# Query parts made a step ahead, and in the dilated units the transposes of the probabilities two steps behind the scores

## The reference

```python
h = _rms_norm(x, norm_attn_g)
qa, ka, va, fa, qb, kb, vb, ga, gb = split(h @ w_in)
oa = _fox_attention(qa, ka, va, log_sigmoid(fa + b_forget))     # 8 heads of 64, causal, forgetting bias
ob = _dilated_mixture(rope(qb), rope(kb), vb)                   # 12 heads: 4 each at dilation 1, 4, 16
mixed = sigmoid(ga) * (oa @ w_branch_a) + sigmoid(gb) * (ob @ w_branch_b)
x = x + mixed @ w_out
x = x + square(relu(_rms_norm(x, norm_mlp_g) @ w_up)) @ w_down
return _rms_norm(x, norm_final_g)
```

## Time and profile before

| | |
|---|---|
| time, median of 3 runs | 1677.96 us (1674.87 to 1681.14) |
| profiled execution, own time | 1677.7 us |
| its span, first to last instruction | 1675.9 us |
| TensorE busy | 1552.0 us, 93% |
| DVE busy | 1094.3 us, 65% |
| ACT busy | 782.0 us, 47% |
| dilated units | about 71 to 383 us of the span |
| forgetting units | about 413 to 690 us |
| granted TensorE clock, mean | 0.98 of full |

### The profile page before, as it was taken

One profiled execution on the slowest core, in us unless ns is written; L12 is line 12 of the kernel. 1 busy time (PEld: TensorE's weight loads), 2 busy tenths in 40 slices (PEclk: granted clock), 3 DMA queues, 4 the chain that ended last, 5 costly groups with the idle time before them and its releaser, 6 DMA issues. The chain is left out here.

```text
span 1675.9 us, 20825 instructions
## 1 busy us (share of the span) xinstructions
PE 1552.0 (93%) x7436; PEld 1277.8 (76%) x7436; DVE 1094.3 (65%) x1775; ACT 782.0 (47%) x1396; POOL 4.1 (0%) x20
## 2 busy tenths in 40 slices
PE   6998888897789998899999999999999899999997
PEld 5777677775677786788888887888888677777776
DVE  5687878866566666523225567666666677777776
ACT  6466666662556656511113454343343444444442
POOL 0000000000000000000000000000000000000000
PEclk9999999999899999999999999999999999999998
DMA  5210100110010201111211543444444784444412
GB/s 176 89 39 26 38 26 26 28 37 13 13 51 26 76 26 36 36 48 44 56 55 55 151 126 94 151 144 167 163 149 151 248 285 138 140 138 144 139 39 101
DMA packets 161584, 154.45 MB, mean 92 GB/s; under 512 B 7048, under 2 KB 126920, under 8 KB 161360
## 3 DMA queue, kind: packets, MB, share of 16 engines
q1 hardware_dynamic: 161488, 153.19, 28.9%
HBM read 115.35 MB, written 37.81 MB: 91 GB/s over the span
## 5 line engine op out<-in xcount | busy, mean ns | idle before, releaser
L942 PE MATMUL ps<-hspl,wsp 128*128 128x512 f32 x1536 | 428.9, 414 | 5.4 <-ACT tmp L1356 3.7
L942 PEld LDWEIGHTS ps<-hspl,wsp 128*128 128x128 f32 x1536 | 270.8, 193 | 52.2 <-ACT tmp L1356 4.6
L1233 PE MATMUL ps<-dn_b,a_hi 128*128 128x512 f32 x896 | 280.0, 394 | 17.5 <-DVE keep L2022 11.8
L898 PE MATMUL ps<-hspl,wsp 128*128 128x512 f32 x960 | 220.7, 390 | 1.4 <-DVE keep L1869 1.4
L1233 PEld LDWEIGHTS ps<-dn_b,a_hi 128*128 128x128 f32 x896 | 168.0, 189 | 59.3 <-issue 24.1
L898 PEld LDWEIGHTS ps<-hspl,wsp 128*128 128x128 f32 x960 | 179.7, 188 | 38.6 <-issue 1.6
L1233 PE MATMUL ps<-dn_b,a_lo 128*128 128x512 f32 x448 | 175.8, 392 | 0.0
L2022 DVE TENSOR_TENSOR keep<-keep,ps 128x512 f32<-128x512 f32 (+1 forms) x144 | 101.5, 713 | 38.2 <-PE ps L1233 24.5
L1233 PE MATMUL ps<-up_b,a_hi 128*128 128x512 f32 x384 | 119.6, 393 | 3.7 <-DVE up_b L2022 2.7
L1855 DVE TENSOR_TENSOR work<-ps,work 128x128 fp32r<-128x128 f32 (+3 forms) x144 | 59.1, 420 | 72.3 <-ACT work L1401 70.2
L1604 ACT ACTIVATE keep<-keep 128x512 f32<-128x512 f32 x64 | 40.5, 633 | 125.9 <-DVE keep L2184 42.8
(11 more groups left out here) (211 smaller groups left out, 2560.8 us busy)
## 6 DMA issues: line engine op xcount, KB each, us to landing
hidden<-keep SPq DMA_DIRECT2D x112, 256.0 KB, 2.2
dn_raw<-hidden SPq DMA_DIRECT2D x56, 512.0 KB, 6.4
raw<-in_w_in SPq DMA_DIRECT2D x47, 512.0 KB, 3.8
a_raw<-in_w_up SPq DMA_DIRECT2D x36, 256.0 KB, 3.0
a_raw<-in_w_down SPq DMA_DIRECT2D x32, 256.0 KB, 3.0
spare<-in_w_down SPq DMA_DIRECT2D x32, 256.0 KB, 4.2
spare<-in_w_up SPq DMA_DIRECT2D x28, 256.0 KB, 3.2
keep<-in_x SPq DMA_DIRECT2D x8, 512.0 KB, 7.0
```

The lines of the kernel that those rows point to most:

```text
L898: ins = pe.matmul(ps[:, cols], w(wp, k), mv(mp, k)[:, cols], start=(k == 0 and n == 0), stop=(k == ks - 1 and n == 2))
L942: ins = pe.matmul(psp(u, g), wsp[c % 2][:, wp, k * P:(k + 1) * P], hspl[:, mp, k, cols], start=(n == 0), stop=(n == 23), skip_group_check= ...
L1233: ins = pe.matmul(o, a_part(n, j, wp, k), b_block(n, j, mp, k), start=(first and k == 0 and m == 0), stop=(k == ks - 1 and m == 2), skip_g ...
```

## The change

No instruction is added or taken away in sum. Three things change.

1. `query_ops(G)` says which query parts a step makes: part 0 of block `B` in step `2B - 3`, part 1 in `2B - 2`, one step ahead of before. A unit's first block is made whole in step 14 and step 13 makes none. On ACT the query part now stands behind `exps` and `probs_hi`. Ahead of the loop one more query part is made.
2. In the dilated units (`late` = 1) the transposes, both parts of the probabilities, the values, the outputs and the values' transposes each move one step back: `transposes(G - 2)` in step `G`, outputs in odd steps instead of even ones, `value_transposes` in step 2 instead of 1.
3. Probabilities of the dilated units have a third buffer, `probs_third`, and `exps(G)` waits for `transposes(G - 3)`. In the forgetting units these things stay.

```diff
@@ -185,6 +185,14 @@
     return [(i - 1, None), (i, None)]
 
 
+def query_ops(G):
+
+    B, n = (G + 1) // 2 + 1, (G + 1) % 2
+    if G % STEPS == 13 or G == STEPS * N_DIL - 1 or B >= BLOCKS * MIX:
+        return []
+    return [(B, 0), (B, 1)] if G % STEPS == 14 or G == STEPS * N_DIL else [(B, n)]
+
+
 def tiles_of(G):
     return key_tiles(G // STEPS, query_tile(G % STEPS))
 
@@ -262,6 +270,7 @@
         fbias = [at(f"fbias{i}", [P, 2, S], F32, 196 + 8 * i) for i in range(2)]
 
         q_fox = at("q_fox", [P, 2, 2, 2 * P], F32R, 192)
+        probs_third = at("probs_third", [P, 2 * P], F32, 92)
         pt_odd = at("pt_odd", [P, 2048], F32R, 128)
 
         up_b = [at(f"up_b{j}", [P, 2, 4, HALF], F32R, 64 + 16 * j) for j in range(3)]
@@ -379,7 +388,7 @@
         def probs(G):
 
             if G < STEPS * N_DIL:
-                return tmp[:, 6, HALF + (G % 2) * 256:HALF + (G % 2 + 1) * 256]
+                return probs_third[:, :] if G % 3 == 2 else tmp[:, 6, HALF + (G % 3) * 256:HALF + (G % 3 + 1) * 256]
             return tmp[:, G % 2, :]
 
 
@@ -1025,22 +1034,23 @@
                         ins.then_inc(vt_done, 1)
 
             def mixer_steps(first, last):
-                for G in range(first, last + 2):
+                late = 0 if first else 1
+                for G in range(first, last + 2 + late):
                     if G < last:
                         scores(G)
                     if G < last:
                         project_part(G, 0)
-                    if first <= G - 1 < last:
-                        transposes(G - 1)
+                    if first <= G - 1 - late < last:
+                        transposes(G - 1 - late)
                     if G < last:
                         project_part(G, 1)
                     if G < last:
                         project_part(G, 2)
-                    if G % 2 and first <= G - 3 < last:
+                    if (G - late) % 2 and first <= G - 3 - late < last:
                         if G % STEPS == 1 and first:
                             inverse_rows(G // STEPS - N_DIL - 1)
-                        values((G - 3) // 2)
-                    if G % STEPS == 1 and G < last:
+                        values((G - 3 - late) // 2)
+                    if G % STEPS == 1 + late and G < last:
                         value_transposes(G // STEPS)
 
             for g in range(6):
@@ -1387,7 +1397,7 @@
             def exps(G):
                 n = len(tiles_of(G))
                 act.wait_ge(max_done, G + 1)
-                after(act, tr_done, units_before(G - 1))
+                after(act, tr_done, units_before(G - 1 if G > STEPS * N_DIL else G - 2))
                 act.activation(probs(G)[:, 0:n * P], psc[G % 2][:, 0:n * P], ACT.Exp,
                                bias=stat(G, 0), scale=-1.0, accum_out=stat(G, 1)).then_inc(exp_done, 1)
 
@@ -1416,24 +1426,25 @@
                 act.copy(o_part[row:row + 64, :], o_bank(B)[64 - row:P - row, :]).then_inc(op_done, 1)
 
             def mixer_steps(first, last):
-                for G in range(first, last + 3):
+                late = 0 if first else 1
+                for G in range(first, last + 3 + late):
                     t, s = divmod(G, STEPS)
                     if group_out(t, s) is not None and G < last:
                         raw_evacuate(t + 1, group_out(t, s))
                     if s == 0 and G > first:
                         raw_evacuate(t, 5 if t < MIX else 3)
-                    if G % 2 == 0 and first <= G - 4 < last:
+                    if (G - late) % 2 == 0 and first <= G - 4 - late < last:
                         if s == 2 and first:
                             inverse_rows(t - N_DIL - 1)
-                        out_part((G - 4) // 2)
-                    if G < last and G // 2 + 1 < BLOCKS * MIX:
-                        query_hi(G // 2 + 1, G % 2)
+                        out_part((G - 4 - late) // 2)
                     if G < last:
                         exps(G)
-                    if first <= G - 1 < last:
-                        probs_hi(G - 1)
+                    if first <= G - 1 - late < last:
+                        probs_hi(G - 1 - late)
                     if G < last:
-                        if s == 1:
+                        for B, n in query_ops(G):
+                            query_hi(B, n)
+                        if s == 1 + late:
                             values_hi(t)
                         if s == (0 if t == N_DIL else 2):
                             split_hi(CH0 + 3 * t + 4)
@@ -1459,6 +1470,7 @@
             query_hi(0, 0)
             query_hi(0, 1)
             raw_evacuate(0, 5)
+            query_hi(1, 0)
             mixer_steps(0, STEPS * N_DIL)
 
 
@@ -1896,22 +1908,24 @@
                 return jobs
 
             def mixer_steps(first, last):
-                for G in range(first, last + 3):
+                late = 0 if first else 1
+                for G in range(first, last + 3 + late):
                     t, s = divmod(G, STEPS)
-                    if G % 2 == 0 and first <= G - 4 < last:
-                        outs((G - 4) // 2)
+                    if (G - late) % 2 == 0 and first <= G - 4 - late < last:
+                        outs((G - 4 - late) // 2)
                     jobs = side_work(G) if G < last else []
                     if G < last:
                         maxes(G)
                     for job in jobs[:1]:
                         job()
-                    if first <= G - 1 < last:
-                        probs_lo(G - 1)
+                    if first <= G - 1 - late < last:
+                        probs_lo(G - 1 - late)
                         if first and G > first and s == 0:
                             inverses(t - N_DIL - 1)
-                    if G < last and G // 2 + 1 < BLOCKS * MIX:
-                        query_lo(G // 2 + 1, G % 2)
-                    if s == 1 and G < last:
+                    if G < last:
+                        for B, n in query_ops(G):
+                            query_lo(B, n)
+                    if s == 1 + late and G < last:
                         values_lo(t)
                     for job in jobs[1:]:
                         job()
@@ -1926,6 +1940,7 @@
             split_lo(4)
             query_lo(0, 0)
             query_lo(0, 1)
+            query_lo(1, 0)
             mixer_steps(0, STEPS * N_DIL)
 
 
```

## The result

The changed kernel takes 1682.94 us (median of 7 runs, 1681.05 to 1688.02), the kernel before beside it 1678.29 us (7 runs, 1673.76 to 1681.14): a ratio of 1.0039, 95% interval 1.0022 to 1.0055. The forecast of no change on the slow side, 1684 us, holds. Not all of its terms do: its two halves, for the dilated and the forgetting units, were off by some 5.5 us each, in opposite directions.

What follows compares the result with a forecast made beforehand. The prediction took the DVE-ACT round trip to bound the dilated units, not TensorE. Its terms, -10.4 + 1.5 + 10.9 + 7.5 + 1.0 - 2.1 - 2.3 = +6.1 on 1677.7 us, gave 1684 us; range 1660 to 1698.

Steps and rivals of the forecast that it cites:

- The thesis: Dilated units: TensorE's 24.3 us of query waits mostly shadow a DVE-ACT loop, which an earlier TensorE doesn't shorten.
- Query part behind the cast on ACT, +10.9: Dilated units: DVE's query part must wait for ACT's later query cast; +10.9 us, bounds 0 and 15.
- Outputs in odd steps, and step 3, +8.5: Dilated units: DVE waits for output parts queued on ACT; +7.5 us for step 9, +1.0 for step 3.
- What an earlier TensorE gives in the dilated units, -4.4: Dilated units: score waits after halved-clock steps go, -2.1 us; step 3's exp no longer stands behind the query cast, -2.3.
- Forgetting units, -10.4 + 1.5: Forgetting units: earlier query parts remove DVE's score waits, -10.4 us; first step and dilated stretch's later drain add +1.5.
- TensorE's waits whole, 1636 us: Both stretches: TensorE's query waits, 41.8 us, come back whole: 1636 us; chance 0.17, from 1636 to 1667.
- Dilated costs hidden, 1667 us: DVE catches up in each unit's last steps, so only the forgetting units' -10.4 stays: 1667 us; chance 0.15.
- The clock, 1701 us: Dilated units: TensorE's idle time gathers at steps 9 and 10, lowering its clock; 17 us more, 1701 us; chance 0.16.

Runs made afterwards that it cites:

- one_behind: q_first_dil with transposes, probabilities, values and outputs one step behind, in two buffers, as before the change; ratio 0.9950 to the kernel before.
- dilated_only: Dilated units as in the change, forgetting units as in the kernel before; ratio 1.0058 to the kernel before.
- outs_behind2: The change with both output halves moved behind in the dilated units, ACT's copy behind its query part; ratio 0.9969 to the kernel before.
- q_first_dil: The change, but ACT makes its query part ahead of the exp in the dilated units; ratio 0.9972 to the kernel before.
- q_first_all: The change, but ACT makes its query part ahead of the exp in all units; ratio 0.9920 to the kernel before.

## Why the prediction was right, and where it was wrong

**The thesis held for the waits it was about.** TensorE's waits for query parts in the dilated units were mostly the shadow of a loop through DVE and ACT. They went from 24.3 to 6.0 us and the stretch grew by 9.7 us. DVE's idle time grew to 79.0 us, where under 60 would have refuted it. By that loop's own account, the idle time ahead of DVE's groups against the earlier trace rows: max 9.9 to 1.1 us, probabilities 36.1 to 30.8, output 12.8 to 17.1, -9.8 in sum, and the query part up to 25.2 from next to nothing. DVE's idle time follows the stretch; TensorE's waits for query parts don't. But not all of the growth is that loop's own: 6.3 of the 9.7 us are slower products on TensorE, for which the sum has no term.

**Query part behind the cast on ACT, +10.9.** Right: 11.9 us between the kernels that differ in it, 9.5 of them idle time. The waits per step were right too (0.39 us for 0.37). Their total was not, 23.0 us instead of 11; since the maxes and probabilities are waited for 14.1 us less, part of it only changed its place.

**Outputs in odd steps, and step 3, +8.5: the waits right, the price not shown.** There are four waits of 1.54 to 1.78 us in step 9 (1.7 forecast), 0.79 in unit 0 (0.7), 1.02 in step 3 (1.2). But other waits for output parts went, and their total is 16.2 us, where the prediction had some 25 (11.9 before). The second step behind as a whole costs 7.1 us, near the 8.5, and that nearness is luck: 6.9 of the 7.1 are slower products, not waits for the output. It was not foreseen that taking the outputs off the loop altogether gives up to 14 us, 8.4 of them by the clock.

**What an earlier TensorE gives in the dilated units, -4.4: the sign right, too small.** With one step behind and the query ahead, the stretch is 336.9 us against 346.9 (means of two kernels each): -10.0. The step that failed is "most others are at the start, before there is a lead". I kept 6.8 of DVE's 8.9 us of waits for scores; in one_behind 1.0 is left:

```profile
L1864 DVE CUSTOM_DVE_ANT_0 ps<-ps,dil_bias 128x128 f32<-128x128 f32 (+1 forms) x96 | 34.7, 361 | 1.9 <-PE ps L991 1.0
```

Of the 10.0 us, 6.8 are TensorE's idle time and 3.2 its busy time; the three falls of the clock in the kernel before, for which the prediction took 2.1 us, are gone in one_behind. The rest was not traced to single waits.

**Forgetting units, -10.4 + 1.5: this term was mis-sized, -3.3 measured.** DVE's waits for scores did fall as forecast, 12.3 to 1.5 us, and with ACT's query ahead the stretch shrinks by 12.0 us (263.2 to 251.2), so the gain was there. The step that failed is the sentence on ACT: that the high query part behind the cast is hidden, because DVE's part of 512 columns is longer. DVE's query part does not wait, but it isn't the only one behind that cast. At the head of the next step stands the emptying of the bank, and TensorE, which now comes early, waits for it: 3.2 us before, 17.0 after. The prediction named who waits for a moved instruction, and left out who waits for what is queued behind it. The Trainium skill, "PSUM — Partial Sum Buffer", section "Engine vs sequencer instructions", has ScalarE's queue as strictly first in, first out; the rows of unit 8 agree, with the bank's copy 0.58 us later for a query cast of 0.41.

**The sum.** -10.4 + 1.5 + 15.0 = +6.1 was forecast. The trace has -3.3 in the forgetting and +9.7 in the dilated stretch, +1.0 ahead of them, and -2.1 behind them, where the code is the same: +5.3. Both halves were some 5.5 us off, in opposite directions. That the sum is closer than its parts is luck.

**The rivals.** TensorE's waits whole, 1636 us: no kernel came near, though the mended one takes 24 us less than before; it gets them only with ACT's query part left ahead of the exp and the transposes one step behind. Dilated costs hidden, 1667 us: excluded by dilated_only. The clock, 1701 us: the mechanism took place, where the prediction had put it, and was priced too high. TensorE's lead does gather its idle time in one piece near step 10, as in unit 2:

```profile
212.82 0.68 PE L1023 MATMUL ps<-work 128*128 128x256 f32 x4 [3.31 <-DVE work L1867]
```

In the dilated loop of the change the clock falls to its lower level six times (at 156, 214, 234, 272, 292 and 330 us), before it three times, and not at all in outs_behind2 and one_behind. Each of the six begins within 1.5 us of the end of a wait of TensorE of 2.1 to 3.3 us: four for the values near step 10, two for the bank at the head of a unit. The rival had ten stretches and 17 us; the trace has three more than before and 6.3 us more of busy time. In the forgetting units it is not the clock that tells the change from what came before: TensorE's busy time there is 230.5 us, 233.6 before.

## What to carry to other kernels

Price a moved wait on the engine whose waits add up to the stretch, not on the busiest one: here TensorE's 41.8 us of waits for DVE were worth 10.0 + 12.0 us once nothing else was moved for the worse, and in the change 18 of them went in the dilated units while the stretch grew by 9.7 us. When an instruction moves within an in-order queue, list what stands behind its new place until the next wait, and ask for each who waits for it. When a change moves several things at once, undo them one at a time: making the query parts a step ahead was worth 22 us here, and what came with it cost 28.7 (ACT's order 11.9 and 9.7, the second step behind 7.1). And divide a stretch into TensorE's busy and idle time before you explain it by waits: where the same products take longer, ask for the clock, and look for the long pieces of idle time ahead of its falls.

## What the hardware showed that was not expected

A wait of 1.14 us left TensorE's granted clock at 1.00 and one of 2.25 us was followed by 4 us at 0.58, at the same place of the program. The wait of 2.26 us in the earlier trace rows was followed by 0.57. So a delay of half a microsecond on ACT was followed by two projection products of 1.22 instead of 0.73 us.

The length of the wait alone does not decide it. In q_first_dil and q_first_all, at the same place of the same code, TensorE waits 2.88 and 2.87 us; over the 4 us from there the granted clock is 0.64 in the one and 1.00 in the other:

```profile
210.27 0.68 PE L1023 MATMUL ps<-work 128*128 128x256 f32 x4 [2.88 <-DVE work L1871]
210.20:214.20 4.00, 3.93 (x15) 3.27 (x16) 3.77 (x11) 2.80 (x7) 0.00 (x0) 0.64 0.01 2
```

```profile
210.83 0.68 PE L1023 MATMUL ps<-work 128*128 128x256 f32 x4 [2.87 <-DVE work L1871]
210.80:214.80 4.00, 3.97 (x21) 3.14 (x22) 3.77 (x10) 2.74 (x7) 0.00 (x0) 1.00 0.01 2
```

What else decides it no run here shows. It is one reason why kernels with the same code in a stretch differ there by up to 2.8 us.
